# Two transformer blocks on one core: banks, queues and slots of the work around the matrix products rearranged

## The reference

```
h = rms_norm(x); proj = h @ w_in                       # 1024 -> 8708 columns
ys = [stick(...), dilated(...), forgetting(...), rms_norm(differential(...))]
branch = einsum('bsnc,ncd->bsnd', ys, w_branch)
x = x + sum(sigmoid(gate_logit) * branch) @ w_out
x = x + square(relu(rms_norm(x) @ w_up)) @ w_down
x = rms_norm(x)
# block two
q, k, v, u = split(rms_norm(x) @ w_in_2)               # 1024 -> 2560 columns
attn = softmax(rope(norm(q)) rope(norm(k)).T) @ v
conv = silu(layer_norm(depthwise_conv(glu(u), 31 taps)))
x = x + concat(attn, conv) @ w_out_2
x = x + (silu(rms_norm(x) @ w_gate) * (rms_norm(x) @ w_up)) @ w_down
```

## Time and profile before

| | |
|---|---|
| median of 3 runs | 812.22 us (812.01 to 813.08) |
| the profiled execution's own time | 809.01 us |
| its span, first to last instruction | 807.2 us |
| TensorE busy | 782.7 us |
| VectorE busy | 477.3 us |
| ScalarE busy | 408.3 us |
| GpSimd busy | 44.2 us |
| granted TensorE clock | 1.00 |

### The profile page before, as it was taken

The page is one execution under the profiler, slowest core; times in us unless marked ns, Lnnn a source line. Parts: engine busy times, 40 slices in busy tenths (PEclk is TensorE's granted clock), DMA queues, the critical chain, the costliest instruction groups (busy, mean ns, idle before and its releaser), DMA issues.

```text
span 807.2 us, 9725 instructions
## 1 busy us (share of the span) xinstructions
PE 782.7 (97%) x3930; PEld 657.4 (81%) x3930; DVE 477.3 (59%) x623; ACT 408.3 (51%) x542; POOL 44.2 (5%) x38
## 2 busy tenths in 40 slices
PE   7999999999999999999999999989999999999998
PEld 5887889878888878888888887767987888888896
DVE  6654364656766877554445448589956654545434
ACT  6565455455656636455444446555556443443341
POOL 1000000000001410000000005011000000000000
PEclk9999999999999999999999999999999999999999
DMA  9842424434445356555655555736123654655341
GB/s 331 319 158 84 151 79 158 149 112 158 156 158 189 124 193 226 198 184 175 208 176 188 180 186 186 283 111 207 56 60 134 224 195 172 207 165 200 104 157 53
DMA packets 68509, 136.25 MB, mean 169 GB/s; under 512 B 2417, under 2 KB 7153, under 8 KB 67825
## 3 DMA queue, kind: packets, MB, share of 16 engines
q1 hardware_dynamic: 68000, 134.44, 49.0%
q10 hardware_dynamic: 464, 1.20, 0.4%
HBM read 134.43 MB, written 1.05 MB: 168 GB/s over the span
## 4 chain that ended last, share of the span: by engine, by line
PE 85%; DVE 9%; ACT 2%; issue 2%; POOL 1%; DMA 1%; SPq 0%; ACTq 0%; DVEq 0%; POOLq 0%
PE b L579 19%; PE b L581 19%; PE b L580 18%; PE SS L579 4%; PE SS L581 4%; PE SS L580 4%; PE TT L548 4%; PE OO L579 2%; PE OO L581 2%; PE OO L580 2%; DVE wlo L1502 2%; DVE ca L1972 1%; PE OO L893 1%; PE SS L662 1%; PE b L719 1%
## 5 line engine op out<-in xcount | busy, mean ns | idle before, releaser
L1502 DVE TENSOR_TENSOR wlo<-raw,whi 128x2048 fp32r<-128x2048 f32 (+2 forms) x123 | 274.2, 2230 | 160.8 <-ACT whi L1061 160.5
L1061 ACT CAST whi<-raw 128x2048 fp32r<-128x2048 f32 (+2 forms) x123 | 227.9, 1854 | 127.5 <-PE b L581 88.0
L579 PE MATMUL b<-whi,Ahi 128*128 128x512 f32 (+2 forms) x568 | 222.2, 391 | 7.4 <-ACT ust L1337 3.4
L581 PE MATMUL b<-whi,Alo 128*128 128x512 f32 (+2 forms) x568 | 215.3, 379 | 0.0
L580 PE MATMUL b<-wlo,Ahi 128*128 128x512 f32 (+2 forms) x568 | 214.7, 378 | 0.0
L579 PEld LDWEIGHTS b<-whi,Ahi 128*128 128x128 f32 x568 | 107.2, 189 | 28.2 <-ACT ust L1337 3.8
L581 PEld LDWEIGHTS b<-whi,Alo 128*128 128x128 f32 x568 | 107.0, 188 | 20.7
L580 PEld LDWEIGHTS b<-wlo,Ahi 128*128 128x128 f32 x568 | 107.4, 189 | 18.3
L579 PE MATMUL b<-whi,Bhi 128*128 128x512 f32 x154 | 60.9, 395 | 0.0
L581 PE MATMUL b<-whi,Blo 128*128 128x512 f32 x154 | 60.0, 390 | 0.0
L580 PE MATMUL b<-wlo,Bhi 128*128 128x512 f32 x154 | 60.0, 390 | 0.0
(11 more groups left out here) (273 smaller groups left out, 1027.0 us busy)
## 6 DMA issues: line engine op xcount, KB each, us to landing
raw<-in_w_in SPq DMA_DIRECT2D x40, 1024.0 KB, 4.9
raw<-in_w_up SPq DMA_DIRECT2D x16, 1024.0 KB, 5.4
raw<-in_w_dn SPq DMA_DIRECT2D x16, 1024.0 KB, 5.0
raw<-in_w_d SPq DMA_DIRECT2D x11, 1024.0 KB, 4.9
raw<-in_w_g SPq DMA_DIRECT2D x10, 1024.0 KB, 4.9
raw<-in_w_u SPq DMA_DIRECT2D x10, 1024.0 KB, 5.0
raw<-in_w_out SPq DMA_DIRECT2D x8, 1024.0 KB, 4.9
raw<-in_w_br SPq DMA_DIRECT2D x4, 1024.0 KB, 4.9
```

Of the source, the lines that this page charges most:

```text
L579: e.matmul(dst, xh, H[:, kc, c0:ce], start=first and kc == krs[0], stop=False)
L581: ins = e.matmul(dst, xl, H[:, kc, c0:ce], start=False, stop=last and kc == krs[-1])
L1061: e.copy(whi[:, s, 0:m], raw[:, r, 0:m]).then_inc(s_hi, 1)
L1502: e.tensor_tensor(wlo[:, s, 0:m], raw[:, r, 0:m], whi[:, s, 0:m].bitcast(F32), ALU.subtract).then_inc(s_lo, 1)
```

## The change

It has these parts.

1. **Slots of block one.** Stick-breaking heads 2 and 3 start a slot later, and `sc` and all behind it come a slot later in every head. In the dilated and forgetting tasks `t`, `pc`, `pv` and `wr` come a slot later; starts of tasks 13 to 23 move by one to two slots; the second pair of chunk 6 and both pairs of chunk 8 move by one slot; `nl` moves a slot nearer to its head; the transposes of the finished halves and the last norm move by one to three slots.
2. **`other_t`.** `sc` and `pt` take the other of banks 5 and 6 where the one whose turn it is is transposed into by a `tp` of the same slot.
3. **Gated branches.** The product of gate and last branch is written back into its bank, and the addition into `mx` reads it from there; the bank is then free after the addition.
4. **Block two's banks.** Chunks alternate between banks 1, 2 and banks 0, 7.
5. **Transfers.** The four transfers of `phases` are issued by SyncE, ahead of the load of the second unit of the output projection; the small casts `identR` and `triR` move from slot 9 to slot 1 of ScalarE.
6. **Smaller ones.** `rturn` alternates between banks 5 and 6; `r0` of VectorE stands ahead of the slot's split; one tap moves from slot 14 to the heads; the first part of the convolution is issued ahead of the first head's scores.

```diff
+P2B = [(1, 2), (0, 7)]
-        s = 4 * c + (4 if first else 5) if c < 8 else 42 if first else 44
+        s = 4 * c + (4 if first else 6 if c == 6 else 5) if c < 8 else 43 if first else 45
-    for h, a in enumerate((8, 9, 13, 14)):
-        for k, name in enumerate(("sz", "sm", "ss", "sc", "su", "sp", "so")):
+    for h, a in enumerate((8, 9, 14, 15)):
+        for k, name in ((0, "sz"), (1, "sm"), (2, "ss"), (4, "sc"), (5, "su"), (6, "sp"), (7, "so")):
-    starts += [40, 41, 43, 44, 46, 46, 48, 48]
-    starts += [50, 50, 53, 53, 56, 56, 59, 59]
+    starts += [40, 41, 43, 44, 46, 47, 49, 50]
+    starts += [51, 51, 54, 54, 57, 57, 60, 60]
-            bg[a - 2].append(("nl", h))
-        names = ("z", "x", "cb", "t", "pc", "pv", "wr") if kind == "diff" else ("z", "x", "t", "pc", "pv", "wr")
+            bg[a - 1].append(("nl", h))
+        if kind == "diff":
+            stages = zip(range(7), ("z", "x", "cb", "t", "pc", "pv", "wr"))
+        else:
+            stages = zip((0, 1, 3, 4, 5, 6), ("z", "x", "t", "pc", "pv", "wr"))
...
-    for s, n in ((10, 7), (12, 2), (14, 4), (18, 2)):
+    for s, n in ((10, 7), (12, 2), (14, 3), (18, 2)):
...
+            if i == unit_of["wo2", 0, 1, 0]:
+                w.wait_ge(s_pad, 1)
+                w.wait_ge(s_ug, 2)
+                for k in range(2):
+                    e.dma_start(hp[64:128, 2 * k, 0:143], odd[0:64, k, 0:143]).then_inc(d_hp, 16)
+                    e.dma_start(hp[0:64, 2 * k + 1, 0:143], odd[64:128, k, 0:143]).then_inc(d_hp, 16)
...
+        def other_t(s):
+            bk = next_t()
+            return 11 - bk if bk in [5 + (QP[i][2] // 2) % 2 for name, i in BG1[s] if name == "tp"] else bk
...
-                    gone[bk] = (s_gm, g + 1)
+                    gone[bk] = (s_mix, 2 * hf + t + 1) if n == 3 else (s_gm, g + 1)
...
-                product(("p2", i, ui, t), Ahi, Alo, 4 * ui, t, lambda c0, t=t: bank[1 + t], ui == 0, ui == 1)
+                bk = P2B[i % 2][t]
+                if ui == 0:
+                    clear(bk)
+                product(("p2", i, ui, t), Ahi, Alo, 4 * ui, t, lambda c0, bk=bk: bank[bk], ui == 0, ui == 1)
+                gone[bk] = (s_ev, 36 + 2 * i + t + 1)
...
-            az(k)
-            tile_part()
             if k:
+                az(k)
+                tile_part()
                 at(k - 1)
+            else:
+                tile_part()
+                az(k)
...
-                elif name == "ug" and i == 1:
-                    phases()
-                    w.wait_ge(d_cs1, 32)
-                    e.copy(identR[:], ident)
-                    e.copy(triR[:], maskF[:, 128:256]).then_inc(s_tri, 1)
...
-            e.tensor_tensor(sg, sg, bk, ALU.mult).then_inc(s_gm, 1)
-            if n == 3:
-                w.wait_ge(s_gm, g + 1)
-                w.wait_ge(s_pm, 4 * hf + 2 + t + 1)
-                e.tensor_tensor(mx, mx, sg, ALU.add).then_inc(s_mix, 1)
+            e.tensor_tensor(bk, sg, bk, ALU.mult).then_inc(s_gm, 1)
+            w.wait_ge(s_gm, g + 1)
+            w.wait_ge(s_pm, 4 * hf + 2 + t + 1)
+            e.tensor_tensor(mx, mx, bk, ALU.add).then_inc(s_mix, 1)
```

More of the change, by code:

```diff
@@ L110, in timetable1 @@
         if kind == "fox" and q == 0:
-            bg[a - 2].append(("nl", h))
-        names = ("z", "x", "cb", "t", "pc", "pv", "wr") if kind == "diff" else ("z", "x", "t", "pc", "pv", "wr")
-        for k, name in enumerate(names):
+            bg[a - 1].append(("nl", h))
[3 more added lines that the diff above has]
+            stages = zip((0, 1, 3, 4, 5, 6), ("z", "x", "t", "pc", "pv", "wr"))
+        for k, name in stages:
             bg[a + k].append((name, n))
@@ L119, in timetable1 @@
     for t in range(2):
[L120 to L125, removed]
+        bg[55].append(("tt", t))
+        bg[56].append(("tu", t))
+        bg[67].append(("dn", t))
+        bg[68].append(("de", t))
+        bg[68].append(("tt", 2 + t))
+        bg[69].append(("tu", 2 + t))
     rank = {"wr": 0, "so": 0, "fq": 0, "nl": 0}
@@ L623, in sz, with sc @@
             gone[bk] = (s_sm, h + 1)
-        def sc(h):
-            bk = tbank["sb", h] = next_t()
+        def sc(h, s):
+            bk = tbank["sb", h] = other_t(s)
             w.wait_ge(d_cs1, 32)
@@ L687, in z, with pt @@
             gone[bk] = (s_zf, n + 1)
-        def pt(n):
+        def pt(n, s):
             nb = blocks_of(n)
@@ L694, in pt @@
                 w.wait_ge(s_e, n + 1)
-            bk = tbank[n] = 5 if nb > 4 else next_t()
+            bk = tbank[n] = 5 if nb > 4 else other_t(s)
             clear(bk)
@@ L752, in stages1 @@
                 elif name == "sc":
-                    sc(i)
+                    sc(i, s)
                 elif name == "sp":
@@ L758, in stages1 @@
                 elif name == "t":
-                    pt(i)
+                    pt(i, s)
                 elif name == "pv":
@@ L876, in rturn @@
             w.wait_ge(s_ra, i + 1)
-            clear(5)
-            turn4(bank[5], rope_buf(i)[0]).then_inc(s_rt, 1)
-            gone[5] = (s_q2, i + 1)
+            clear(5 + i % 2)
+            turn4(bank[5 + i % 2], rope_buf(i)[0]).then_inc(s_rt, 1)
+            gone[5 + i % 2] = (s_q2, i + 1)
         def conv(m):
@@ L946, in _ @@
                 stages2(4 * i + q)
-        gone[1], gone[2] = (s_ev, 45), (s_ev, 46)
         n_conv = [0]
@@ L1336, in evac2 @@
                 o = V2[:, t, :]
-            e.mul(o, bank[1 + t], r).then_inc(s_ev, 1)
+            e.mul(o, bank[P2B[i % 2][t]], r).then_inc(s_ev, 1)
         def gs(t):
@@ L1353, in r2 @@
             w.wait_ge(s_rt, i + 1)
-            src = bank[5].rearrange("p (k q) -> p k q", k=4)
+            src = bank[5 + i % 2].rearrange("p (k q) -> p k q", k=4)
             ts = slice(128 * t, 128 * t + 128)
@@ L1361, in r2 @@
             e.mul(qk2T[64:128, 4:8, ts], src[64:128], 0.125).then_inc(s_q2, 1)
[L1363 to L1369, removed]
         def am(h):
@@ L1416, in _ @@
                 stages2(4 * i + q)
+                if 4 * i + q == 1:
+                    w.wait_ge(d_cs1, 32)
+                    e.copy(identR[:], ident)
+                    e.copy(triR[:], maskF[:, 128:256]).then_inc(s_tri, 1)
                 if 4 * i + q == 7:
@@ L1992, in stages2 @@
             for name, i in BG2[s]:
-                if name == "r0":
-                    r0(i)
-                elif name == "ra":
+                if name == "ra":
                     ra(i)
@@ L2004, in _ @@
                         r1(h)
+                    elif name == "r0":
+                        r0(h)
                 if i == 0 and q == 0:
```

7 lines of the change are left out of this document (3 added, 4 removed).

## The result

The changed kernel takes 800.15 us (median of 4 runs, 797.38 to 801.09), the kernel before in the same comparison 812.12 us (808.88 to 813.08): a ratio of 0.9854, 95% interval 0.9817 to 0.989. The forecast was 801.5 us. Two more comparisons gave 800.21 us (0.9848, 0.9833 to 0.9862) and 799.28 us (0.9845, 0.9822 to 0.9869). The profiled execution took 797.38 us; its clock was 1.00.

What follows compares the result with a forecast made beforehand. TensorE was taken as the bound, busy 782.7 of 807.2 us, with VectorE bounding as much between 540 and 560. Gains of 3.6 + 1.0 + 6.1 = 10.7 us took 812.2 to 801.5 us; range 798.0 to 805.8.

Steps and rivals of the forecast that it cites:

- Attention: Block one's attention: 6.1 us from removed gaps, less 0.3 and 2.2, gives a gain of 3.6 us.
- All five gaps: TensorE gaps in block one's attention at 66.78, 71.97, 108.82, 149.08 and 171.50: all go, worth 6.1 us.
- The new wait: Near 200 us, TensorE waits at a `pv` for ScalarE's copy, behind task 17's `x` and a cast: loses 2.2 us.
- the turns: Attention: TensorE turns between large products and small work in ten more slots, costing 0.3 us, bounds 0 and 1.1.
- The rival in which this wait was covered: Attention, slot 53: TensorE does not wait for the exponentials or `pc`; 12.9 us gained, 799.3 us, chance 0.2.
- Gated branches: Output projection's gap at 289.25 shrinks by 1.0 us as additions reading a bank take 0.69; bounds 0.5 and 1.4.
- Block two: From 506.14 on: 5.2 us by the transposes at 555.01 plus 0.9 at the heads, 6.1 us; bounds 4.5 and 7.1.
- the first gap: Block two at 506.14, chunk 0's read-out waiting for the root: goes whole by the new banks, 2.6 us.
- The wait of the first `rturn`: Block two, before the first rotary transposes: TensorE waits for VectorE's `r1`, some 1.8 us.
- The rival in which VectorE gives less: Block two gives 4.5 us and one more wait like 2.2 stands in attention: 805.3 us, chance 0.2.
- The other side: Slots 41 to 57: ScalarE's queue becomes the bound, TensorE loses 13.2 us, time 814.7 us; chance 0.06.
- the second gap: Block two at 533.46, chunk 2's read-out behind `phases`: goes, worth 3.6 us, but TensorE can't keep it all.

Runs made afterwards that it cites:

- the last run: Only the slots of block one and `other_t` (parts 1 and 2 of the change) added to the kernel before: median 807.42 us, ratio 0.9944.
- the heads later: Changed kernel with differential tasks 17 and up, the transposes of the finished halves and the last norm one slot later: median 795.53 us, ratio 0.9794 to the kernel before.
- both moves: Changed kernel with the heads later and five convolution taps moved from block two's slot 10 to behind the last head: median 794.55 us, ratio 0.9788 to the kernel before.

## Why the prediction was right

**Attention.** Forecast 3.6 us, measured 3.9. All five gaps went. The new wait stood where it was put, with the chain that was written down, 1.94 us printed for 2.2 forecast. What is left, 3.9 and about 2.1 for the wait, is 6.0 for 5.8 forecast (6.1 less 0.3 for the turns). The rival in which this wait was covered is out: the copy ahead of the cast showed that the exponentials and the cast were both in front of it.

**Gated branches.** Forecast 1.0, measured 1.2. The addition fell from 1.69 to 0.69, and the split behind it was held as foreseen, by 0.4. In the second half the addition and the split together gave 1.00 - 0.41 = 0.6 (0.55 forecast), so the first half handed down 0.6 (0.45 forecast); its own lines say the same, an addition 0.66 shorter and a split held by 0.06. One figure of the working is misread: 1.69 us from 285.21 reach 286.90, 0.55 behind GpSimd's end at 286.35 and not 0.69. The forecast does not use it. Writing the product into a bank costs 0.68 us, as much as into SBUF: the bound of 0.07 on four of them was not needed. The fixed cost that the Trainium skill gives an instruction that reads PSUM (VectorE: DVE Perf Modes, section on the TRN2 errata) does not show in an addition that takes 0.69 us from either side.

**Block two.** Forecast 6.1, measured 6.2: 2.4 at the first gap, 2.6 counted to the start of slot 5, where the slower first matmuls behind the gap are over (2.6 forecast), the transposes of 555.01 earlier by 5.3 (5.2 forecast, counted from the end of the branches), and 0.9 more at the heads (0.9). The wait of the first `rturn` was forecast at 1.8 with its ends and printed 1.68. This is where the forecast could have failed: the printed gaps of 2.33 and 3.38 suggest some 6 us, and VectorE's row without idle time said that 1.8 would be kept back. The rival in which VectorE gives less is out.

**The other side.** ScalarE's queue did not become the bound: one `pc` came behind a late `x`, not five. The reason given, that the turn freeing `Sb` stands at least a slot ahead of `x` but for tasks 16 and 17, held.

**The level.** The sum was 10.7 us; the traces show 11.2 and 0.4 of start-up. The median lies 1.35 us below the forecast. 0.5 of it is the sum and 0.4 the start-up of the profiled execution. The last 0.4 is the step that carried the 3.2 us between the profiled execution of before and its median over to the new kernel as a constant: here that distance is 2.8. It is not noise without a cause. The profile of before had a clock of 1.00; of the 28 later executions of that kernel whose clock is on record one stood at 1.000, with 809.03 us, and the others at 0.992 to 0.998, with 810.00 to 813.69 us. The landing of the input has a part in it that only profiled executions show (1.1 of the 2.7 us between the first two profiles of the changed kernel). The changed kernel has fewer long waits, and its medians lie 1.9 to 2.8 us above its first profile at full clock. The landing alone moved the start of slot 4 between 21.22 and 22.98 us in the thirteen traces, so that two totals agree within 1.35 us is partly luck. What bears the forecast out is the stages, each within 0.3 us.

## What to carry to other kernels

When a gap is removed, follow the engine that releases the next dependent step and look at its idle time ahead of it: the second gap here needed both shared banks and transfers ahead of a read-out, and what could be kept of it stood in VectorE's row, not in TensorE's. The wait in the relay through in-order queues went away by a slot more between its ends (2.2 us in the trace, 4.7 in the median), not by swapping two entries in the middle, which handed it to the next step. Work that bounds a stretch has to leave the stretch: five taps moved within it gave 0.1 us, moved behind it 1.8.

## What the runs showed of the hardware

TensorE's clock can fall behind a wait of about 2 us. It is not tied to one place: a clock below 1.00, half for most of it, stood for some 3 to 7 us right behind waits of 1.94, 1.96, 1.97, 2.33, 3.37 and 3.96 us in the runs above (for 3.37 from the wait's last microsecond on), and by the starts of the slots it cost 0.6 to 2.2 us each time (2.2 behind 3.37 us: from slot 12 to 15 of block two 11.33 us in the last run, 9.16 before). Nor does it come every time: waits of 1.94, 2.33 and 3.38 us stand in the first two profiles with the clock at 1.00, and one of 1.97 in that of the last branch gated into SBUF. Up to 788 us no other stretch of 2 us in the thirteen traces has a clock below 0.97. In the runs that had no wait above 1.7 us (the heads later, and both moves) the mean clock of all eight executions was 0.999 or 1.000, and the four times of each lie within 1.4 us. The executions of before that were timed beside the changed kernel's third comparison show the steps:

```
810.00 us 0.998    810.23 us 0.998    810.25 us 0.998    812.23 us 0.994    812.34 us 0.994
812.59 us 0.994    812.86 us 0.994    813.26 us 0.994    813.69 us 0.992
```

Three levels of clock, and the times in their order. In the traces one fall goes with a mean clock of 0.997 or 0.998 (five of them) and two falls with 0.994 (the last run). That the levels of the executions without a trace count such falls is inferred from this and not shown. A wait that prints 2 us cost 1.6 to 1.7 us more where the clock fell behind it, and between the medians with and without it lie 4.7, so the gain of taking it away is not to be read from one profile at full clock. What decides in which executions the clock falls stays open: no run here varied the length of one wait alone.
